# RWKV-7 mixer of a hybrid backbone on eight cores: forward and backward scan packed onto 128 partitions

## What is computed

```python
def rwkv7_scan(r, w, k, v, a, b, s0):
    '''S_t = S_{t-1} diag(w_t) + (S_{t-1} a_t) b_t^T + v_t k_t^T ;  y_t = S_t r_t.'''
...
    for d in range(2):
        yc, s_ctx = rwkv7_direction(f_ctx, d, s0)
        yl, _ = rwkv7_direction(f_lat, d, s_ctx)
        y_ctx = y_ctx + yc
        y_lat = y_lat + yl
```

## Time and profile before

| | us |
|---|---|
| median of six runs | 21473.61 |
| lowest and highest of them | 21323.16, 21841.33 |
| the profiled execution | 21181.76 |
| its span on the slowest core (core 5) | 21180.4 |
| the shortest span of a core | 20961.3 |

### The profile page before, as it was taken

One profiled execution on the slowest core, in us unless ns is written; L12 is line 12 of the kernel. 1 busy time (PEld: TensorE's weight loads), 2 busy tenths in 40 slices (PEclk: granted clock), 3 DMA queues, 4 the chain that ended last, 5 costly groups with the idle time before them and its releaser, 6 DMA issues.

```text
span 21180.4 us, 244978 instructions; the slowest of 8 cores (20961.3 to 21180.4 us)
## 1 busy us (share of the span) xinstructions
PE 12160.2 (57%) x68280; PEld 6378.3 (30%) x68280; DVE 8761.0 (41%) x18358; ACT 3902.2 (18%) x10036; POOL 2142.5 (10%) x3033
## 2 busy tenths in 40 slices
PE   5635524334443447445453344433524999999997
PEld 1222313222332223223141233222312444444443
DVE  1164215454455335127314544545345334444443
ACT  1142002222222210114002222222211001111110
POOL 0000211111111110100211111111110000000000
PEclk8856655555555579775675555555557889999998
DMA  4401420000000221330230000000121212222222
GB/s 146 121 26 32 144 60 1 5 5 5 6 1 5 79 78 35 119 94 7 80 124 17 5 6 2 4 5 5 42 83 34 36 30 36 36 42 37 36 38 53
DMA packets 495908, 913.75 MB, mean 43 GB/s; under 512 B 79441, under 2 KB 281458, under 8 KB 486470
## 3 DMA queue, kind: packets, MB, share of 16 engines
q1 hardware_dynamic: 278016, 643.71, 9.3%
q0 software_dynamic: 204112, 229.20, 6.9%
q10 hardware_dynamic: 12480, 25.17, 0.4%
HBM read 952.75 MB, written 174.37 MB: 53 GB/s over the span
## 4 chain that ended last, share of the span: by engine, by line
PE 44%; DVE 20%; DMA 15%; issue 10%; ACT 6%; POOL 4%; DVEq 1%; SPq 1%; ACTq 0%; POOLq 0%
PE psb L659 8%; PE psb L662 8%; PE psb L672 8%; PE psb L1222 3%; PE psb L1216 2%; PE psb L1217 1%; PE psb L1155 1%; PE psb L1122 1%; DVE acc L685 1%; PE psb L1200 1%; PE psb L1000 1%; DVE rjunk L609 1%; PE psb L939 1%; DMA mu<-rw_shift 1%; PE psb L804 1%
## 5 line engine op out<-in xcount | busy, mean ns | idle before, releaser
L680 DVE SCALAR_TENSOR_TENSOR acc<-psb,gates,acc 128x512 f32<-128x512 f32 x1760 | 1321.1, 751 | 332.3 <-PE psb L672 181.9
L659 PE MATMUL psb<-fhT,w1b_571 128*128 128x512 bf16 x3584 | 872.9, 388 | 56.2 <-DMA w2b_575<-moe_w 56.2
L662 PE MATMUL psb<-fhT,w3b_574 128*128 128x512 bf16 x3584 | 876.2, 389 | 0.0
L659 PE MATMUL psb<-fhT,w1b_572 128*128 128x512 bf16 x3584 | 875.9, 389 | 0.0
L662 PE MATMUL psb<-fhT,w3b_573 128*128 128x512 bf16 x3584 | 872.5, 388 | 0.0
L666 DVE TENSOR_TENSOR gT<-psb,sil_578 128x512 bf16<-128x512 f32 x448 | 309.8, 692 | 1317.1 <-PE psb L659 922.2
L1103 PE MATMUL psb<-ident_b,rw_TB 64*64 64x64 bf16 x2160 | 125.8, 237 | 1259.8 <-DVE rw_TB L1182 1038.9
L666 DVE TENSOR_TENSOR gT<-psb,sil_579 128x512 bf16<-128x512 f32 x448 | 309.9, 692 | 1293.4 <-PE psb L659 918.9
L672 PE MATMUL psb<-w2b_575,gT 128*128 128x512 bf16 x3584 | 807.9, 389 | 33.3 <-DVE gT L666 33.3
L672 PE MATMUL psb<-w2b_576,gT 128*128 128x512 bf16 x3584 | 803.5, 388 | 33.7 <-DVE gT L666 33.7
L665 ACT ACTIVATE sil_578<-psb 128x512 f32<-128x512 f32 x448 | 267.5, 597 | 2970.4 <-PE psb L659 2970.4
(11 more groups left out here) (1142 smaller groups left out, 27647.0 us busy)
## 6 DMA issues: line engine op xcount, KB each, us to landing
w1b_571<-moe_w POOLq DMA_DIRECT2D x28, 1024.0 KB, 8.2
w3b_573<-moe_w POOLq DMA_DIRECT2D x28, 1024.0 KB, 8.3
w2b_575<-moe_w POOLq DMA_DIRECT2D x28, 1024.0 KB, 8.2
w1b_572<-moe_w POOLq DMA_DIRECT2D x28, 1024.0 KB, 8.3
w3b_574<-moe_w POOLq DMA_DIRECT2D x28, 1024.0 KB, 8.3
w2b_576<-moe_w POOLq DMA_DIRECT2D x28, 1024.0 KB, 8.2
rwraw<-u_rwT SPq DMA_DIRECT2D x44, 576.0 KB
adaw_7<-ada_w SPq DMA_DIRECT2D x12, 2048.0 KB, 13.5
```

The lines of the kernel that those rows point to most:

```text
L659: em.op("pe", lambda e, k=k, p1=p1, fc=fc, s=s, n=n, b=b: e.matmul(p1[:, 0:n], w1b[b][:, k, fc * 128:(fc + 1) * 128], hT[:, k, t0 + s:t0 + ...
L662: em.op("pe", lambda e, k=k, p3=p3, fc=fc, s=s, n=n, b=b: e.matmul(p3[:, 0:n], w3b[b][:, k, fc * 128:(fc + 1) * 128], hT[:, k, t0 + s:t0 + ...
L680: em.op("dve", lambda e, ps=ps, asl=asl, gcol=gcol: e.scalar_tensor_tensor(asl, ps[:], gcol, asl, ALU.mult, ALU.add), reads=[dp, dgates, d ...
```

## The change

Both directions go into one stream of instructions. On the 128 partitions of a tile, 0 to 63 hold the forward direction, 64 to 127 the backward one. The backward chunks are written in reversed order when the operands are made (`rviews`, an access pattern with a negative step), so that chunk number ci means the ci-th step of both directions. `ARP`, `BP`, `KP` hold both directions side by side along the free axis; a product of two of them is 128 by 128 or 128 by 256, and the masks `rw_M2`, `rw_MP` put zeros where the directions cross, so that all later products are block-diagonal. V and U become block-diagonal tiles (`Vblk`, `Ub`), zeroed once outside the blocks. The state stays 64 partitions high, with the directions side by side (`S2`, `Sb2`). The banks of the scan are three (`bankI`, `bankJ`, `bankC`) where they were four, and `psum()` rotates over five. At the end of a head the backward half of Y is moved to partitions 0 to 63 by a DMA and added.

The diff, cut to its core:

```diff
...
+    M2[0:64, 0, 0, :] = (t64 > s64); M2[0:64, 1, 0, :] = (t64 >= s64)
+    M2[64:128, 0, 1, :] = (t64 < s64); M2[64:128, 1, 1, :] = (t64 <= s64)
+    MPm[0:64, 0:64] = (np.arange(64)[None, :] < np.arange(64)[:, None])
+    MPm[64:128, 64:128] = (np.arange(64)[None, :] > np.arange(64)[:, None])
...
+            Y2 = self.sb(st, "rw_Y2", [128, R_, 64]); dy = Dep()
...
+            ARP = self.sb(st, "rw_ARP", [64, R_, 2, 2, 64], BF16); dARP = Dep()
+            BP = self.sb(st, "rw_BP", [64, R_, 2, 64], BF16); KP = self.sb(st, "rw_KP", [64, R_, 2, 64], BF16); dBP = Dep(); dKP = Dep()
+            TBP = self.sb(st, "rw_TBP", [64, R_, 2, 64], BF16); dTBP = Dep()
+            Bh2 = self.sb(st, "rw_Bh2", [128, R_, 64], BF16); Kh2 = self.sb(st, "rw_Kh2", [128, R_, 64], BF16); dBh2 = Dep(); dKh2 = Dep()
+            Vblk = self.sb(st, "rw_Vblk", [128, R_, 128], BF16); dVblk = Dep()
+            gCP = self.sb(st, "rw_gCP", [64, R_, 2]); dgCP = Dep()
...
+            MB = [self.sb(st, f"rw_MB{i}", [128, 256], BF16) for i in range(2)]; dMB = [Dep(), Dep()]
+            MK = [self.sb(st, f"rw_MK{i}", [128, 256], BF16) for i in range(2)]; dMK = [Dep(), Dep()]
...
+            Rm = [self.sb(st, f"rw_R{i}", [128, 128], BF16) for i in range(2)]; dRm = [Dep(), Dep()]
...
+            Ub = [self.sb(st, f"rw_Ub{i}", [128, 128], BF16) for i in range(2)]; dUb = [Dep(), Dep()]
+            M2, dM2 = self.load_const(st, "rw_M2"); MP, dMP = self.load_const(st, "rw_MP")
+            em.op("pool", lambda e: e.memset(Vblk[:], 0.0), writes=[dVblk])
...
+            bankI = (self.ps[5], self.psd[5]); bankJ = (self.ps[6], self.psd[6]); bankC = (self.ps[7], self.psd[7])
...
+            def rviews(ap3, d):
+                if d == 0:
+                    return [(slice(0, R_), ap3)]
+                base = ap3[:, 0, :]
+                def rev(cstart, n):
+                    return bass.AP(base.tensor, base.offset + cstart * 64, [list(base.ap[0]), [-64, n], [1, 64]])
+                return [(slice(0, NCC), rev(NCC - 1, NCC)), (slice(NCC, R_), rev(R_ - 1, R_ - NCC))]
...
                     for j in range(nb):
-                        em.op("pe", lambda e, pb=pb, j=j, c0=c0: e.transpose(pb[0:64, j * 64:(j + 1) * 64], src3[:, c0 + j, :], idb[0:64, 0:64]), reads=[dsrc, self.d_ident_b], writes=[dp])
+                        em.op("pe", lambda e, pb=pb, j=j, c0=c0: e.transpose(pb[:, j * 64:(j + 1) * 64], TBP[:, c0 + j, :, :].rearrange("p d t -> p (d t)"), idb[0:64, 0:64]), reads=[dTBP, self.d_ident_b], writes=[dp])
...
+                for d in range(2):
+                    for (rs, vin) in rviews(T23, d):
+                        em.op("act", lambda e, rs=rs, vin=vin, d=d: e.activation(TBP[:, rs, d, :], vin, AF.Copy), reads=[dT2], writes=[dTBP])
...
+                    pv = pb[:, 0:nb * 64].rearrange("p (c k) -> p c k", k=64)
+                    em.op("act", lambda e: e.activation(Vblk[0:64, c0:c0 + nb, 0:64], pv[0:64], AF.Copy), reads=[dp], writes=[dVblk])
+                    em.op("act", lambda e: e.activation(Vblk[64:128, c0:c0 + nb, 64:128], pv[64:128], AF.Copy), reads=[dp], writes=[dVblk])
...
+                    for (rs, kkv), (_, t1v) in zip(rviews(v3(kk), d), rviews(T13, d)):
+                        em.op("dve", lambda e, rs=rs, kkv=kkv, t1v=t1v, d=d: e.scalar_tensor_tensor(ARP[:, rs, 0, d, :], kkv, -1.0, t1v, ALU.mult, ALU.mult), reads=[dkk, dT1], writes=[dARP])
+                    em.op("act", lambda e: e.activation(T1[0:64, :], T2[:], AF.Exp, scale=-CD), reads=[dT2, dARP], writes=[dT1])
...
+                    for (rs, rv), (_, t1v) in zip(rviews(v3(r_), d), rviews(T13, d)):
+                        em.op("dve", lambda e, rs=rs, rv=rv, t1v=t1v, d=d: e.tensor_tensor(ARP[:, rs, 1, d, :], rv, t1v, ALU.mult), reads=[dr_, dT1], writes=[dARP])
+                        em.op("pool", lambda e, rs=rs, t1v=t1v, d=d, gsel=gsel: e.tensor_copy(gCP[:, rs, d], t1v[:, :, gsel]), reads=[dT1], writes=[dgCP])
...
-                    em.op("dve", lambda e, o=o: e.tensor_tensor(o["bdb"][:], bd[:], T2[:], ALU.mult), reads=[dbd, dT2], writes=[o["dbdb"]])
-                    em.op("pool", lambda e, o=o: e.tensor_tensor(o["kdb"][:], kd[:], T2[:], ALU.mult), reads=[dkd, dT2], writes=[o["dkdb"]])
...
-                    transp_chunks(TB3, dTB, o["Bh"], o["dBh"])
...
-                    transp_chunks(TB3, dTB, o["Kh"], o["dKh"])
...
+                    for (rs, bv), (_, kv), (_, t2v) in zip(rviews(v3(bd), d), rviews(v3(kd), d), rviews(T23, d)):
+                        em.op("dve", lambda e, rs=rs, bv=bv, t2v=t2v, d=d: e.tensor_tensor(BP[:, rs, d, :], bv, t2v, ALU.mult), reads=[dbd, dT2], writes=[dBP])
+                        em.op("pool", lambda e, rs=rs, kv=kv, t2v=t2v, d=d: e.tensor_tensor(KP[:, rs, d, :], kv, t2v, ALU.mult), reads=[dkd, dT2], writes=[dKP])
+                gbc2 = gCP[:].rearrange("p r (d o) -> p r d o", o=1).to_broadcast([64, R_, 2, 64])
+                em.op("dve", lambda e: e.tensor_tensor(TBP[:], BP[:], gbc2, ALU.mult), reads=[dBP, dgCP, dVblk], writes=[dTBP])
+
+                def b_evac(c0, nb, pb, dp):
...
+                em.op("dve", lambda e: e.tensor_tensor(TBP[:], KP[:], gbc2, ALU.mult), reads=[dKP, dgCP, dBh2], writes=[dTBP])
+
+                def k_evac(c0, nb, pb, dp):
+                    em.op("act", lambda e: e.activation(Kh2[:, c0:c0 + nb, :], pb[:, 0:nb * 64].rearrange("p (c k) -> p c k", k=64), AF.Copy), reads=[dp], writes=[dKh2])
...
-                    em.op("pe", lambda e: e.matmul(bk[0:64, 0:128], BT, AR[:, c, :], start=True, stop=True), reads=[o["dbdb"], dAR], writes=[dbk])
...
+                    em.op("pe", lambda e: e.matmul(bk[:, 0:256], bp, arp, start=True, stop=True), reads=[dBP, dARP], writes=[dbk])
+                    em.op("pe", lambda e: e.matmul(bk[:, 256:512], kp, arp, start=True, stop=True), reads=[dKP, dARP], writes=[dbk])
...
-                    em.op("dve", lambda e: e.tensor_tensor(MB[b][:], bk[0:64, 0:128], m2[:], ALU.mult), reads=[dbk, dmk], writes=[dMB[b]])
...
+                    em.op("dve", lambda e: e.tensor_tensor(MB[b][:], bk[:, 0:256], M2[:], ALU.mult), reads=[dbk, dM2], writes=[dMB[b]])
+                    em.op("dve", lambda e: e.tensor_tensor(QP[q0][:, 128:256], bj[:, 0:128], MP[:], ALU.mult), reads=[dbj, dMP], writes=[dQP[q0]])
+                    em.op("dve", lambda e: e.tensor_tensor(MK[b][:], bk[:, 256:512], M2[:], ALU.mult), reads=[dbk, dM2], writes=[dMK[b]])
...
-                    em.op("pool", lambda e: e.tensor_tensor(Rm[b][:], MB[b][:, 0:64], idb[0:64, 0:64], ALU.add), reads=[dMB[b], self.d_ident_b], writes=[dRm[b]])
+                    em.op("pool", lambda e: e.tensor_copy(QP[q0][:, 0:128], MB[b][:, 0:128]), reads=[dMB[b]], writes=[dQP[q0]])
...
+                        pq, dpq = bj[:, 128:384], dbj
+                            em.op("pe", lambda e, cur=cur: e.matmul(pq[:, 0:128], QP[cur][:, 128:256], QP[cur][:, 0:128], start=True, stop=True), reads=[dQP[cur]], writes=[dpq])
+                        em.op("pe", lambda e, cur=cur: e.matmul(pq[:, 128:256], QP[cur][:, 0:128], QP[cur][:, 128:256], start=True, stop=True), reads=[dQP[cur]], writes=[dpq])
+                        em.op("act", lambda e, nxt=nxt, lo=lo: e.activation(QP[nxt][:, lo:256], pq[:, lo:256], AF.Copy), reads=[dpq], writes=[dQP[nxt]])
...
+                        em.op("pe", lambda e, nxt=nxt: e.matmul(pr[:, 0:128], QP[nxt][:, 128:256], Rm[b][:], start=True, stop=True), reads=[dQP[nxt], dRm[b]], writes=[dpr])
+                        em.op("dve", lambda e: e.tensor_tensor(Rm[b][:], pr[:, 0:128], Rm[b][:], ALU.add), reads=[dpr, dRm[b]], writes=[dRm[b]])
...
+                    em.op("pe", lambda e: e.matmul(pX, ap_, Sbc[:], start=True, stop=False), reads=[dARP, dSbc], writes=[dbc])
+                    em.op("pe", lambda e: e.matmul(pX, MK[b][:, 0:128], Vblk[:, ci, :], start=False, stop=True), reads=[dMK[b], dVblk], writes=[dbc])
...
+                    em.op("act", lambda e: e.activation(Xs[b][0:64, :], pX[0:64, 0:64], AF.Copy), reads=[dbc], writes=[dXs[b]])
+                    em.op("act", lambda e: e.activation(Xs[b][64:128, :], pX[64:128, 64:128], AF.Copy), reads=[dbc], writes=[dXs[b]])
...
+                    em.op("pe", lambda e: e.matmul(pU, Rm[b][:], Xs[b][:], start=True, stop=True), reads=[dRm[b], dXs[b]], writes=[dbc])
...
+                    em.op("act", lambda e: e.activation(Ub[b][0:64, 0:64], pU[0:64, :], AF.Copy), reads=[dbc], writes=[dUb[b]])
+                    em.op("act", lambda e: e.activation(Ub[b][64:128, 64:128], pU[64:128, :], AF.Copy), reads=[dbc], writes=[dUb[b]])
...
+                    em.op("pe", lambda e: e.matmul(pS, Bh2[:, ci, :], Ub[b][:], start=True, stop=False), reads=[dBh2, dUb[b]], writes=[dbc])
+                    em.op("pe", lambda e: e.matmul(pS, Kh2[:, ci, :], Vblk[:, ci, :], start=False, stop=True), reads=[dKh2, dVblk], writes=[dbc])
```

(9 more changed lines are left out.)

214 lines of the change are left out of this document (87 added, 127 removed).

## The result

| | kernel before | changed kernel |
|---|---|---|
| median, us | 21492.47 (20 runs) | 21896.97 (10 runs) |
| the profiled execution's span, us | 21180.4 | 21869.3 |
| instructions of PE, products | 68280 | 56616 |
| of DVE | 18358 | 14902 |
| of ACT | 10036 | 7840 |

Ratio of the times, after to before: **1.0278, 95% interval 1.0214 to 1.0342**. The two medians lie 1.9% apart: they are of all runs, and the ratio leaves out those that a lower granted clock on part of the cores made longer. The forecast was 22,065 us, +2.75%, with a range of 21,780 to 22,400. Between 17% (PE) and 27% (POOL) of the instructions of each engine are gone, and the time is longer.

The account below looks back on a forecast made before the run. The scan was taken to be bound by the latency of one series, the second direction hidden in it. Scan +505 us and preparation with heads' ends +86 gave +591 on the median 21,473.6: 22,065 us (+2.8%), range 21,780 to 22,400.

Parts of the forecast that it names:

- a round: One round of the scan's series for R, square to next square: 1.95 us, against 1.61 before.
- start of a chunk: In the scan, from the last product with R of one chunk to the next chunk's first square: 2.39 us.
- a chunk: One scan step, between two products for U: 11.03 us, 1.17 more than 9.86; +505 us in all.
- V: Preparation: one copy becomes three and 5 evacuations become 10, and the normalization waits: +5.5 us a head.
- direction 0: Preparation: its multiplies by gC, transposes and evacuations move behind direction 1, whose kd starts sooner: -13.6 us a head.
- direction 1: Preparation, from the exponential's end to the first scan product: 24.7 us for 17.75, +7.0 us a head.
- end of a head: After the scan, transfer of the backward half to partitions 0 to 63 and one add: +8.3 us a head.
- One stream faster: Boundary of two rounds in the scan: the second direction's lag goes, chunk 9.06 us, time 21,214 us; chance 7%.
- Width free: Scan: width and lag cost nothing, chunk unchanged, only preparation counts, 21,560 us (+0.4%); chance 5%.
- Clock: Scan: PE's clock rises from 1.2 to 2.4 GHz, saving about 0.95 us a chunk, 21,655 us; chance 6%.
- DVE's queue: First two rounds: DVE's six small operations between adds of R become the bound, +0.45 us a chunk, 22,260 us; chance 12%.
- Tile to 128 partitions: Skill's rule taken at its word: half the instructions in half the scan's time, 19,414 us; chance 2%.

Follow-up runs that it names:

- The last run: Changed kernel with the series packed without zero blocks, two chunks in flight, R's product in the other bank, and a second bank for the chain: 19,820 us, 0.922.

## Why the prediction was right

Direction and mechanism held, and the size in the main; that the total came out so near is partly luck (below). By its own steps, for one head of the profiled pair (from the first product for U of one head to that of the next 661.2 us before, 723.2 after, +62.0; the sum had +49.3):

| step | forecast, us | measured, us |
|---|---|---|
| a round | 1.95 | 1.91 to 1.99 |
| start of a chunk, product with R to first square | 2.39 | 2.64 |
| last round up to its product | 0.84 | 0.84 |
| a chunk | 11.03 (+1.17) | 11.30 (+1.44) |
| V | +5.5 | +5.8 |
| direction 0 | -13.6 | -13.5 |
| direction 1 | +7.0 | +6.9 |
| end of a head | +8.3 | +9.2 |

- **The path.** That no engine fills the scan and one series' latency sets its pace was the step on which everything rests. One round less takes one round off each chunk; one direction less takes 0.21; a second chunk in flight takes 2.76 off each.
- **The widths.** They came from rows of other lines (a mask of 128 columns, an evacuation of 512) and held to 0.02 us for each engine. That partitions cost nothing was argued from ACT's row of 512 columns, which itself had made the slope; ACT's 0.38 for 128 by 256 bears it out.
- **The start of a chunk was mis-sized**, by 0.25 us or 108 us in all. The sum spaced the products in X and the first products by their columns and left out that PE doesn't load weights ahead across a change of their shape. The five S and Y products that were said to end before the first product with R do not quite: it starts at 3513.53, 0.11 later than ACT's hop allows, so the first round is 1.99. The other rounds were 0.02 to 0.04 under the forecast and gave some of it back. The chunk shown takes 11.24; the remaining 0.06 of the mean come from seven of the 35 chunks, which took 11.4 to 11.9.
- **The end of a head** was 0.9 short: the transfer and its add are 7.8, but the state operations of the last chunk, two halves one after the other, take 1.4 more than before, which was counted nowhere.
- **DVE and POOL.** That POOL keeps its place at the seam was taken by the order of readiness. It holds, by 0.34 us: POOL starts at 3995.28, DVE at 3995.62, and DVE's 7.38 end 2.4 after POOL's end.
- **The sum of both.** The steps of the table come to 36 x 1.44 + 8.4 = 60.2 of the 62.0; where the rest lies is open. Twelve times 62.0 are 744 us, the spans of this pair of executions differ by 689, the forecast had 591, and the runs say 2.8%, near 597. The two pages are single executions, and the stages beside the scan differ by some tens of us. That the forecast total is nearer to the runs than its terms are to this pair is luck: the terms were 12.7 a head short.
- **The rivals.** One stream faster: excluded by the run with one direction. Width free: excluded by the rows of a round. Clock: 0.50 in both. DVE's queue: the rival put the six operations at 1.9 against 1.67 free; they take 1.67 (3514.19 to 3515.86), so they just fit, which nothing in the sum had shown. They cost nothing as long as the square waits for the add, and 0.26 to 0.48 us a chunk as soon as it doesn't (a round of 1.53 or 1.74 for 1.27 and 1.26). "Tile to 128 partitions" at its word would have given 19,414. The last run's 19,820 come near it, by overlap, in a layout that does stand on 128 partitions; no run put two chunks in flight in the kernel before, so what the height adds to that stays open.

## What to carry to other kernels

Where a loop's engines are all below two thirds busy and one chain of steps repeats, packing removes instructions that nobody waits for and widens those that somebody waits for: look for a second independent chain, or for a wait that only exists because two results share a bank, which is tracked as one. If tiles are stacked on the partitions, keep them stacked (two small products on two halves) rather than block-diagonal: here the zeros cost about 0.2 us in a round of 1.93. And cost an edit at the border of two iterations step by step, since that is where the estimates went wrong.

## What was not expected of the hardware

Behind a product of 128 columns, PE's next product starts 0.20 to 0.25 us later if the shape of its weights is another (64*128, 128*128 and 128*64 in turn), with the same shape 0.05 to 0.15. Two products of 64 by 64 on the lower and the upper half of the partitions take together 0.26 us where one takes 0.23 and two on the same half 0.28. The expert stage, untouched by any edit, took longer at a lower granted clock with the same 22,400 products:

```profile
15900.00:21860.00 5960.00, 4982.10 (x22400) 2225.59 (x22400) 2470.54 (x3222) 671.06 (x1029) 280.54 (x252) 0.89 0.23 45
```

```profile
15100.00:21440.00 6340.00, 5341.59 (x22400) 2309.13 (x22400) 2472.82 (x3222) 670.78 (x1029) 282.89 (x253) 0.84 0.22 42
```

The first line is of the changed kernel (0.89), the second of the one with four rounds (0.84): 380 us, nearly half of the 816 that the round less took off, come and go there, and so the distances in the scan carry the verdicts above. Why the clock was lower in that run stays open.
